# A float32 transformer stack on one core: where the matmul operands start in SBUF is moved, most of all in the 272-token phases

## What is computed

```
for l in range(2):                       # first block, T = 272
    h = h + 0.5 * swiglu(rmsnorm(h), gate, up, down)
    h = h + hybrid_mixer(rmsnorm(h))     # 36 column blocks of w_in, attention, conv, w_out
    h = h + 0.5 * swiglu(rmsnorm(h), gate, up, down)
h = rmsnorm(h)[:, 16:]                   # from here on 256 tokens
x = x + 0.5 * swiglu; x = x + diff_attention; x = x + 0.5 * swiglu
x = x + 0.5 * swiglu; x = x + retention;      x = x + 0.5 * swiglu
```

## Time and profile before

| | |
|---|---|
| median of 2 runs | 2177.12 us (2177.0 to 2177.25) |
| profiled execution | 2176.64 us, span 2174.8 us |
| PE / PEld busy | 2164.0 us / 2147.4 us |
| DVE / ACT / POOL busy | 1472.5 / 1202.7 / 282.7 us |
| DMA | 386.57 MB, mean 178 GB/s |

### The profile page before, as it was taken

How to read it: one execution, slowest core, us unless ns; L and a number is a source line. 1 busy time by engine, 2 the same in 40 slices (tenths; PEclk the granted TensorE clock), 3 DMA queues, 4 the chain that set the end, 5 groups by cost and what they waited for, 6 DMA issues and landing times.

```text
span 2174.8 us, 48311 instructions
## 1 busy us (share of the span) xinstructions
PE 2164.0 (100%) x18136; PEld 2147.4 (99%) x18136; DVE 1472.5 (68%) x2242; ACT 1202.7 (55%) x1752; POOL 282.7 (13%) x328
## 2 busy tenths in 40 slices
PE   8999999999999999999999999999999999999999
PEld 8999999999999999999999999999999999999999
DVE  6655998665566579876657657976656656686663
ACT  6444786544444368855545546865455535565552
POOL 0001661100100136220020011010010010101000
PEclk9999999999999999999999999999999999999999
DMA  6554435555455554456655655355655655445563
GB/s 234 178 188 166 162 118 174 173 174 196 154 178 185 182 163 143 148 182 193 204 178 195 202 188 169 117 184 193 206 173 197 212 177 179 156 159 190 193 218 129
DMA packets 100401, 386.57 MB, mean 178 GB/s; under 512 B 11312, under 2 KB 12464, under 8 KB 100304
## 3 DMA queue, kind: packets, MB, share of 16 engines
q1 hardware_dynamic: 99648, 383.89, 53.6%
q0 software_dynamic: 368, 1.26, 0.2%
q10 hardware_dynamic: 288, 0.12, 0.0%
HBM read 384.18 MB, written 1.05 MB: 177 GB/s over the span
## 4 chain that ended last, share of the span: by engine, by line
PE 97%; DVE 2%; ACT 1%; issue 0%; DMA 0%; ACTq 0%
PE bank L411 30%; PE bank L403 30%; PE bank L410 30%; PE bank L757 1%; PE bank L1044 1%; PE bank L1043 1%; PE bank L1045 1%; DVE wlo L426 1%; PE bank L1090 0%; PE bank L707 0%; PE bank L738 0%; PE bank L934 0%; PE bank L937 0%; PE bank L936 0%; PE bank L903 0%; ACT whi L419 0%
## 5 line engine op out<-in xcount | busy, mean ns | idle before, releaser
L403 PE MATMUL bank<-u,whi 128*128 128x256 f32 (+2 forms) x3776 | 1065.5, 282 | 7.1 <-DVE u L464 7.1
L411 PE MATMUL bank<-u,wlo 128*128 128x256 f32 (+1 forms) x3776 | 1062.5, 281 | 0.0
L410 PE MATMUL bank<-u,whi 128*128 128x256 f32 (+1 forms) x3776 | 1059.0, 280 | 0.0
L426 DVE TENSOR_TENSOR wlo<-raw,whi 128x1024 fp32r<-128x1024 f32 (+1 forms) x677 | 892.5, 1320 | 186.6 <-ACT whi L419 186.1
L419 ACT ACTIVATE whi<-raw 128x1024 fp32r<-128x1024 f32 (+1 forms) x677 | 743.7, 1112 | 197.0 <-PE bank L411 176.3
L403 PEld LDWEIGHTS bank<-u,whi 128*128 128x128 f32 x3776 | 710.4, 188 | 8.4 <-DVE wlo L426 7.1
L411 PEld LDWEIGHTS bank<-u,wlo 128*128 128x128 f32 x3776 | 711.6, 188 | 0.0
L410 PEld LDWEIGHTS bank<-u,whi 128*128 128x128 f32 x3776 | 710.6, 188 | 0.9 <-issue 0.2
L403 PE MATMUL bank<-hid,whi 128*128 128x256 f32 (+1 forms) x1408 | 394.2, 280 | 0.0
L410 PE MATMUL bank<-hid,whi 128*128 128x256 f32 (+1 forms) x1408 | 394.2, 280 | 0.0
L411 PE MATMUL bank<-hid,wlo 128*128 128x256 f32 (+1 forms) x1408 | 394.1, 280 | 0.0
(11 more groups left out here) (299 smaller groups left out, 2199.4 us busy)
## 6 DMA issues: line engine op xcount, KB each, us to landing
raw<-w SPq DMA_DIRECT2D x552, 512.0 KB, 3.4
raw<-w SPq DMA_DIRECT2D x128, 704.0 KB, 4.8
h<-xT SPq DMA_DIRECT2D x4, 272.0 KB, 5.0
outT<-h SPq DMA_DIRECT2D x8, 128.0 KB, 5.0
consts<-cst POOLq DMA_DIRECT2D x1, 576.0 KB, 4.6
dist<-cst POOLq DMA_DIRECT2D x1, 192.0 KB, 3.0
rdist<-cst POOLq DMA_DIRECT2D x1, 192.0 KB, 3.5
sgain<-small POOLq DMA_DIRECT2D x1, 145.5 KB, 5.1
```

The lines of the kernel that those rows point to most:

```text
L403: pe.matmul(out[:, cut:cols], w, x[:, cut:cols], start=first, stop=False, skip_group_check=True)
L410: pe.matmul(out, w_h, x_lo, start=False, stop=False, skip_group_check=True)
L411: return pe.matmul(out, w_l, x_hi, start=False, stop=last, skip_group_check=True)
L426: dve.tensor_tensor(weights(1, n), raw[:, n % RING, 0:COLS[n]].rearrange("p (k c) -> p k c", c=128), weights(0, n), ALU.subtract).then_inc ...
```

## The change

The tiles of `u` at 272 columns now stand `TILE_STEP` = 320 floats (1280 bytes) apart, and the weight tiles of those panels 128 floats (512 bytes), so that neither moves within a panel. Each panel of a 272-token phase starts in its ring slot at an offset of 0, 16, 32 or 48 floats, which `place_of` computes apart for whi and wlo: in the feed-forward phases a pair of distances for each of the four ring slots (`FFN_DISTANCES`, in units of 64 bytes), in the mixers a pair for each of panels 1 to 16 that runs through all sixteen pairs (`GRID`), and (1, 1) for the others. In phases 1, 3 and 4 the low part of `u` is shifted by 128, 192 and 64 bytes; in phases 0, 2 and 3 `HID_PLACE` shifts `hid` by 56 floats, and its low part by 32, 0 and 48 more. Retention's cuts are made at (5, 1) and (5, 2) where (5, 0) was cut. Lambda's product and sum are made at the start of the first mixer, with `gsq` and `gssq` as their buffers, and `rat_hi` and `rat_lo` lie in the tail of `u`.

```diff
-RY_PAD, GAP_STEP, HID_STEP = 144, 144, 320
-U_PLACE = {0: (48, 0), 1: (48, 0), 2: (48, 0), 3: (48, 0), 4: (48, 0), 5: (48, 0), 6: (48, 0), 8: (48, 0), 9: (48, 0), 10: (48, 0), 11: (48, 0), 12: (48, 0), 7: (48, 0)}
-HID_PLACE = {0: (24, 0), 2: (24, 0), 3: (24, 0), 5: (24, 0), 7: (24, 0), 9: (24, 0), 10: (24, 0), 12: (24, 0)}
+RY_PAD, GAP_STEP, TILE_STEP = 144, 144, 320
+U_PLACE = {0: (48, 0), 1: (48, 32), 2: (48, 0), 3: (48, 48), 4: (48, 16), 5: (48, 0), 6: (48, 0), 8: (48, 0), 9: (48, 0), 10: (48, 0), 11: (48, 0), 12: (48, 0), 7: (48, 0)}
+HID_PLACE = {0: (56, 32), 2: (56, 0), 3: (56, 48), 5: (24, 0), 7: (24, 0), 9: (24, 0), 10: (24, 0), 12: (24, 0)}
...
-BEHIND_TERMS = [(0, 1), (0, 2), *((t, c) for t in range(1, RT_HEADS + 1) for c in (0, 1)), (RT_HEADS, 5), (RT_HEADS + 1, 0)]
+BEHIND_TERMS = [(0, 1), (0, 2), *((t, c) for t in range(1, RT_HEADS + 1) for c in (0, 1)), (RT_HEADS, 5), (RT_HEADS + 1, 1), (RT_HEADS + 1, 2)]
...
+FFN_DISTANCES = {0: ((0, 1), (0, 3), (1, 0), (1, 2)), 2: ((1, 3), (2, 1), (2, 3), (3, 0)),
+                 3: ((1, 1), (3, 3), (2, 2), (0, 0))}
+GRID = [(p, q) for p in range(4) for q in range(4)]
+MIX_DISTANCES = [(1, 1), *GRID, *(((1, 1),) * 19)]
+AT_PLACE = {y: (1 + (48 - place[0]) // 16) % 4 for y, place in U_PLACE.items()}
+
+def place_of(part, n):
+    y = max(i for i in range(len(PHASES)) if BASE[i]["P"] <= n)
+    j = n - BASE[y]["P"]
+    if COLS[n] != K8 or y > LAST_MIX:
+        return 0
+    if PHASES[y] == "mix":
+        if j >= 36:
+            return META if y == LAST_MIX else 0
+        want = MIX_DISTANCES[j][part] + (y == LAST_MIX and j >= 20)
+    else:
+        want = FFN_DISTANCES[y][j % RING][part]
+    return 16 * ((want - AT_PLACE[y]) % 4)
...
-        u = sb("u", [128, 2 * KD * T + 64], f32r)
+        u = sb("u", [128, 2 * KD * TILE_STEP + 48], f32r)
...
-        lam_in = sb("lam_in", [128, 4, 64])
-        lam_p = sb("lam_p", [128, 2, 64])
...
-            hid = sb("hid", [128, 2 * FT * HID_STEP + 96], f32r, area)
+            hid = sb("hid", [128, 2 * FT * TILE_STEP + 144], f32r, area)
...
-            rat_hi = sb("rat_hi", [128, 384], f32r, area)
-            rat_lo = sb("rat_lo", [128, 384], f32r, area)
+            rat_hi, rat_lo = (u[:, 2 * KD * TILE_STEP - 384 * i:2 * KD * TILE_STEP - 384 * (i - 1)] for i in (2, 1))
...
-            step = GAP_STEP if n < BASE[LAST_MIX + 1]["P"] and COLS[n] == K8 else 128
-            at = META if BASE[LAST_MIX]["P"] + 36 <= n < BASE[LAST_MIX + 1]["P"] else 0
+            step = GAP_STEP if in_mixer_end(n) else 128
+            at = place_of(part, n)
```

More of the change, by code:

```diff
@@ L141, with in_mixer_end @@
 DA_PANELS = [(part, n) for part, n in DA_PANELS if 0 <= n < DA_HEADS]
-RY_PAD, GAP_STEP, HID_STEP = 144, 144, 320
-U_PLACE = {0: (48, 0), 1: (48, 0), 2: (48, 0), 3: (48, 0), 4: (48, 0), 5: (48, 0), 6: (48, 0), 8: (48, 0), 9: (48, 0), 10: (48, 0), 11: (48, 0), 12: (48, 0), 7: (48, 0)}
-HID_PLACE = {0: (24, 0), 2: (24, 0), 3: (24, 0), 5: (24, 0), 7: (24, 0), 9: (24, 0), 10: (24, 0), 12: (24, 0)}
+RY_PAD, GAP_STEP, TILE_STEP = 144, 144, 320
+U_PLACE = {0: (48, 0), 1: (48, 32), 2: (48, 0), 3: (48, 48), 4: (48, 16), 5: (48, 0), 6: (48, 0), 8: (48, 0), 9: (48, 0), 10: (48, 0), 11: (48, 0), 12: (48, 0), 7: (48, 0)}
+HID_PLACE = {0: (56, 32), 2: (56, 0), 3: (56, 48), 5: (24, 0), 7: (24, 0), 9: (24, 0), 10: (24, 0), 12: (24, 0)}
 CUTS = (0, 252, 128, 0)
-BEHIND_TERMS = [(0, 1), (0, 2), *((t, c) for t in range(1, RT_HEADS + 1) for c in (0, 1)), (RT_HEADS, 5), (RT_HEADS + 1, 0)]
+BEHIND_TERMS = [(0, 1), (0, 2), *((t, c) for t in range(1, RT_HEADS + 1) for c in (0, 1)), (RT_HEADS, 5), (RT_HEADS + 1, 1), (RT_HEADS + 1, 2)]
+def in_mixer_end(n):
+    return any(BASE[y]["P"] + IN_PANELS <= n < BASE[y + 1]["P"] for y, kind in enumerate(PHASES) if kind == "mix")
+FFN_DISTANCES = {0: ((0, 1), (0, 3), (1, 0), (1, 2)), 2: ((1, 3), (2, 1), (2, 3), (3, 0)),
[15 more added lines that the diff above has]
+    return 16 * ((want - AT_PLACE[y]) % 4)
 def build(nc, w8, w11, xT, small, cst, lam, outT):
@@ L223, in build @@
             gssq = sb("gssq", [128, T], f32, area)
+            lam_in = gsq[:, :, :].rearrange("p a t -> p (a t)")[:, 0:256].rearrange("p (a b) -> p a b", b=64)
+            lam_p = gssq[:, 0:128].rearrange("p (a b) -> p a b", b=64)
         with ExitStack() as area:
@@ L378, in u_at @@
         def u_at(y, part, k, c0=None, c1=T):
-            return tile_of(u, KD, width(y), U_PLACE[y], y, part, k, first_col(y) if c0 is None else c0, c1)
+            step, first = TILE_STEP if y <= LAST_MIX else SEQ, first_col(y)
+            at = (part * KD + k) * step + sum(U_PLACE[y][:part + 1])
+            return u[:, at + (0 if c0 is None else c0 - first):at + c1 - first]
         def hid_at(y, part, f):
-            return tile_of(hid, FT, HID_STEP if y <= LAST_MIX else SEQ, HID_PLACE[y], y, part, f, first_col(y), T)
+            return tile_of(hid, FT, TILE_STEP if y <= LAST_MIX else SEQ, HID_PLACE[y], y, part, f, first_col(y), T)
         def width(y):
@@ L1695, in mix @@
                     dve.wait_ge(const_loaded, CONST_LOADS * 16)
+                    dve.tensor_tensor(lam_p[:, :, :], lam_in[:, 0:4:2, :], lam_in[:, 1:4:2, :], ALU.mult)\
+                       .then_inc(lam_step, 1)
+                    dve.wait_ge(lam_step, 1)
+                    dve.tensor_reduce(lam2[:, 0:2], lam_p[:, :, :], AX.X, ALU.add).then_inc(lam_step, 1)
                     dve.tensor_copy(ones_r[:, :], ones_f).then_inc(const_r, 1)
@@ L2082, in _ @@
                 elif kind == "final":
[L2084 to L2087, removed]
                     dve.tensor_scalar(sub_gain, sub_raw, 1.0 - LAM_INIT, None, ALU.mult).then_inc(lam_step, 1)
```

## The result

The change makes the kernel 1.1% slower: 2201.94 us (2201.75 to 2202.13, two runs) against 2177.12 us, a ratio of 1.0113 with a 95% interval of 1.0096 to 1.0129. That is +24.8 us where +12.8 was forecast: inside the range, on the forecast's side of the old time, and twice as much as its sum.

What follows compares the result with a forecast made beforehand. The prediction took TensorE's matmul count times pitch as the bound. Its terms, 11.1 + 0.4 + 1.7 - 0.4 = +12.8 us on 2176.64, gave 2189.4, forecast as 2190 us, with 2170 to 2204 us for 8 in 10.

Steps and rivals of the forecast that it cites:

- What bounds the kernel: Whole kernel: TensorE, busy 2164.0 of 2174.8 us; time is the number of matmuls times their pitch.
- `hid` at 256 columns: 2640 matmuls go from distance 64 to 128 and fall to the slow level: +11.1 us, bounds 0 to +16.4.
- `u` at 272: 4512 matmuls lose their walk and get sixteen pairs of distances: -19.9 to +9.9 us, taken as 0.
- `hid` at 272: 1584 matmuls leave distance 64 and take the pitch of `u`, 124.4 ns: +1.7 us, bounds -5.2 to +5.2.
- First `u` panels behind `hid`: Four phases following `hid` at 256 columns start slow for one panel until their cuts: +0.4 us.
- Retention's cuts: The two cuts turn retention's last six panels clean: -0.4 us; +0.3 if they do nothing.
- `ry` and differential attention: `ry` goes from 64 to 128, slow already, -1.6 to +0.8 us, taken as 0; `qk` and `ao` stay slow.
- Lambda on VectorE: First mixer: 0.57 us of VectorE work goes in ahead of the casts, covered by waits: 0, at most 0.6 us.
- 128 is clean too: `hid` at 256 columns keeps the clean pitch at distance 128: 2178.5 us, 2172 to 2184; chance 0.20.
- Places mean nothing: Read ports are independent, levels come from the phase after a stop, all stretches keep their pitch: 2176.7 us; chance 0.12.
- Faster: At 272 columns some distances avoid collision, half of 6096 matmuls reach 120.0 ns: 2165 us with `hid` clean; chance 0.09.
- Worse: Distances 0 and 128 collide throughout, `hid` at 119.5 ns, 272-column stretches at 126.6: 2210 us, or 2202; chance 0.11.

Runs made afterwards that it cites:

- experiment 1: The changed kernel with 64 bytes of padding ahead of `hid`, so that `hid`, `ry`, `qk`, `ao` and `dy` start in their line as before the change: 2184.87 us.
- experiment 2: The kernel before with `hid`'s first tile in the 256-column phases 16 floats lower, at distance 128 instead of 64: 2191.7 us, ratio 1.0065.
- experiment 7: The padded, all-64 kernel with the mixers' weight tiles at the change's places and `u`'s low part shifted by 0 and 192 bytes: 2172.88 us.
- Experiment 8: The changed kernel with only `u`'s places taken back to distance 64, `hid` and `ry` left where the change put them, no pad: 2194.2 us.
- experiment 5: The kernel before with retention's cuts at (5, 1) and (5, 2) instead of (5, 0), nothing else: 2175.38 us, ratio 0.9992.
- experiment 3: The kernel before with 64 bytes of padding ahead of the first buffer, all tensors moved and all distances kept: 2177.55 us, ratio 1.0.
- experiment 4: The kernel before with `hid` at another set of distances in each of the five 256-column phases: 2192.15 us.
- experiment 6: The changed kernel with 64 bytes of padding and every distance at 64: 2171.7 us, ratio 0.9976.

## Why the prediction held, and where its sum was short

- **What bounds the kernel** was right: TensorE without a stop, time as count times pitch. VectorE, ScalarE and DMA played no part.
- **`hid` at 256 columns: the step that decided, right in kind, short in size.** Forecast +11.1 us, measured +14.1; experiments 1 and 2 show it from both sides (-17.1 us with all of the area's tensors, +14.4 with `hid` alone). The row that I leaned on was no row for 128: by the table `qk` is at 64, and 128 comes out only as the distance of its next weight tile from the tile that is moving. That the term came out near has luck in it. I took the slow level, 117.5, as what a bad distance gives. It isn't: 117.3 to 117.9 is the level that clean places fall to by history, and distance 128 has its own pitch, 118.7, from the first matmul on. It lay inside the bounds, 0.8 ns below the upper one.
- **`u` at 272: the other term that was mis-sized.** I let the ends cancel at 0; it cost 5.3 us, and 1.2 more in the mixers. The lower end, 120.0, was an estimate from clock and columns, and no set of 64 came near it (experiment 7). With (64, 64, 64) the best that any panel showed, a spread could hardly win, and the row that said so was before me: `hid`, constant at 64, ran 1.1 ns below `u`. I read it for the panels that keep 64 and not against those that leave it. Experiment 8 gives 7.7 us back by `u`'s places alone, though `hid` behind it lost 2.3.
- **`hid` at 272**: forecast +1.7, measured +2.3, by (0, 128, 0), (0, 0, 0) and (0, 64, 0).
- **First `u` panels behind `hid`, +0.4**: did not come. From one `hid` to the next, phases 7 and 10 take 120.95 and 120.39 us in the change against 120.88 and 120.47 before.
- **Retention's cuts, -0.4**: the step works (experiment 5), and with the area put back the phase takes 152.39 us up to `ry` against 152.74 before, the 0.4 us forecast. In the change itself earlier panels fell to the slow level (11.8 us / 101 = 116.8 from 1925), and it takes 153.37, +0.6 us. That this is the shifted area follows from experiment 1; which of its tensors does it was not tried.
- **`ry` and differential attention, 0**: +0.4 and +0.7. I had called `ry` "slow already". By experiments 1 and 5 it was clean by its place, and slow by how the stream reached it. In the change the cuts brought the stream to it clean, and distance 128 took that back.
- **Lambda on VectorE, 0**: right. VectorE's timeline after, with the two instructions in the place foretold, and no wait of TensorE near it:

```profile
212.06 1.21 DVE L457 TENSOR_TENSOR wlo<-raw,whi 128x1024 fp32r<-128x1024 f32 x1
213.19 0.28 DVE L1727 TENSOR_TENSOR gssq<-gsq 128x128 f32<-128x128 f32 x1
213.51 0.29 DVE L1730 TENSOR_REDUCE lam<-gssq 128x2 f32<-128x128 f32 x1
...
214.46 0.44 DVE L1706 TENSOR_TENSOR proj<-bank,R 128x272 f32<-128x272 f32 x1
```

Taken together, the sum was 12.3 us short of the 25.1: 7.1 of it lie in `u` and `hid` at 272 and in the mixers, 3.0 in `hid` at 256, 1.6 in the other terms (2.1 in differential attention, retention and `ry`, less 0.5 for the first panels and the rest), and 0.6 in the start, which isn't the change's.

**The rivals.** "128 is clean too" falls with experiment 2. "Places mean nothing" falls with it as well: one table entry, 64 bytes, 14.4 us. The Trainium skill, SBUF — State Buffer, "Who interferes with whom", says that TensorE's read ports are independent and that it never waits on anyone; the pitches here depend on how the two operands stand to each other, so what the prediction drew from the rule, that their distance means nothing, doesn't hold for this stream of weight loads and matmuls. "Faster" falls with experiment 7, as far as one panel of each set can show. "Worse" wasn't reached, but its mechanism is the larger part of what I was short of: 272-column sets do reach 126 to 129. The 109 and 116 ns that the prediction took from the Trainium skill's TensorE: Matmul & The Clock Gate, "Back-to-back issue gap", are there the gap of an isolated matmul and not that of a stream with weight loads; the lowest steady pitches of any run here are 113.3 and 123.3.

**What stays open.** Experiments 1 to 3 and 7 show that the distance acts, not how. I take it for a conflict between the weight load's reads and the moving operand's, but no run shows those reads apart. Nor is it known what picks one of a set's two pitches: the same stop in `ry` left them apart in two kernels. And since the `dw` panels run at 113.3 or 117.8 at 192, it is open whether `hid` at 192 could be clean too.

## What to carry to other kernels

When TensorE is busy for the whole span, compare its pitch between stretches of equal shape, and read off from the built program how far the weight tile stands from the moving tile; a buffer that grows by 64 bytes can cost more than an instruction that is added. Before spreading places in the hope of a better mean, look for a stretch with one constant place: if that is already the fastest, put everything there. After any edit that changes a buffer's size, look up the starts of the tensors behind it, and pad them back.

## What the runs showed of the hardware that I had not expected

- At 256 columns one set of distances (64 in all three products) runs at 113.3 ns, five others at 117.6 to 119.8 (experiment 4) and 128 at 118.7; at 272, 123.3 against 124 to 128.8, but for one panel of (192, 128, 0). Moving both operands by the same 64 bytes changes nothing (experiment 3).
- The same instructions at the same distances have two steady pitches: 113.3 and 117.8 at 256, 124.5 and 128.8 at 272. Cuts in the stream brought the lower one back at 256 (experiment 5), and a short stop in `ry` was followed by the upper one in one kernel and by the lower one in four (experiment 6).
- From 256 to 272 columns the best pitch rises by 10.0 ns, where the prediction had reckoned with 6.7.
